# A two-block transformer forward pass on one core, with and without the products of zeros at its stage boundaries

## What is computed

```python
for layer in range(2):                               # first block
    h = rmsnorm(x, norm_mix)
    qkv, gates = split(h @ w_in)
    o = [window_attention(qkv), stick_breaking(qkv), moba(qkv)]
    x = x + sum(sigmoid(g + b) * (o_i @ w_branch_i)) @ w_out
    h = rmsnorm(x, norm_ffn)
    u_a, u_v = split(causal_conv(h @ w_up))
    x = x + (silu(u_a) * u_v) @ w_down
x = rmsnorm(x, norm_final)
for l in range(2):                                   # second block
    mix = concat(retention(x), mla_attention(x), mlstm(x)) @ w_out_2
    x = layer_norm(alpha * x + mix)
    f = swiglu(x) if l == 0 else moe_swiglu(x)       # 8 experts, top 2
    x = layer_norm(alpha * x + f)
```

## Time and profile before

| | us |
|---|---|
| median of 3 runs | 2707.37 |
| the runs | 2696.85, 2707.37, 2708.14 |
| the profiled execution, from first to last instruction | 2697.0 |

### The profile page before, as it was taken

One profiled execution on the slowest core, in us unless ns is written; L12 is line 12 of the kernel. 1 busy time (PEld: TensorE's weight loads), 2 busy tenths in 40 slices (PEclk: granted clock), 3 DMA queues, 4 the chain that ended last, 5 costly groups with the idle time before them and its releaser, 6 DMA issues.

```text
span 2697.0 us, 38879 instructions
## 1 busy us (share of the span) xinstructions
PE 2569.2 (95%) x13770; PEld 2161.1 (80%) x13770; DVE 1873.7 (69%) x2141; ACT 1443.7 (54%) x1434; POOL 36.6 (1%) x46
## 2 busy tenths in 40 slices
PE   8979999998899999999999988999999999999997
PEld 7758799896688998868998767878787878788785
DVE  4536688745466876745445647888888888888888
ACT  4454444444544443533433434767677777776764
POOL 0010000000000000000000000000000000000000
PEclk9989999998899999979999788999999999999999
DMA  6305545441254554423553225989898989898986
GB/s 255 141 20 199 187 174 186 155 168 67 100 197 157 188 186 162 153 78 135 184 184 137 94 78 202 369 313 375 316 368 323 348 324 356 328 345 335 341 336 261
DMA packets 81898, 595.27 MB, mean 221 GB/s; under 512 B 9088, under 2 KB 9232, under 8 KB 10256
## 3 DMA queue, kind: packets, MB, share of 16 engines
q1 hardware_dynamic: 80624, 583.64, 58.3%
q0 software_dynamic: 1184, 10.45, 1.0%
HBM read 593.01 MB, written 1.05 MB: 220 GB/s over the span
## 4 chain that ended last, share of the span: by engine, by line
issue 69%; PE 24%; DVE 3%; DVEq 1%; ACT 1%; POOL 1%; DMA 0%; ACTq 0%; POOLq 0%
PE bank L291 6%; PE bank L292 6%; PE bank L293 6%; PE bank L377 2%; DVEq L571 1%; DVE w_lo L579 1%; PE bank L402 1%; PE bank L387 1%; DVE probs L642 0%; ACT w_hi L459 0%; DVE x_tok L1741 0%; POOL probs L738 0%; PE bank L403 0%; PE bank L337 0%; POOL small L730 0%
## 5 line engine op out<-in xcount | busy, mean ns | idle before, releaser
L579 DVE TENSOR_TENSOR w_lo<-raw,w_hi 128x2048 fp32r<-128x2048 f32 x550 | 1249.4, 2290 | 431.6 <-ACT w_hi L459 391.9
L459 ACT CAST w_hi<-raw 128x2048 fp32r<-128x2048 f32 x550 | 1050.4, 1913 | 506.9 <-PE bank L293 494.3
L291 PE MATMUL bank<-w_hi,hT_hi 128*128 128x512 f32 (+3 forms) x1360 | 538.1, 396 | 19.1 <-DVE w_lo L579 12.5
L293 PE MATMUL bank<-w_hi,hT_lo 128*128 128x512 f32 (+3 forms) x1360 | 526.1, 387 | 0.0
L292 PE MATMUL bank<-w_lo,hT_hi 128*128 128x512 f32 (+3 forms) x1360 | 525.6, 386 | 0.0
L291 PE MATMUL bank<-hT_hi,w_hi 128*128 128x256 f32 (+1 forms) x1568 | 451.1, 288 | 5.1 <-DVEq L597 4.5
L293 PE MATMUL bank<-hT_hi,w_lo 128*128 128x256 f32 (+1 forms) x1568 | 445.1, 284 | 0.0
L292 PE MATMUL bank<-hT_lo,w_hi 128*128 128x256 f32 (+1 forms) x1568 | 445.1, 284 | 0.0
L291 PE MATMUL bank<-w_hi,oT_hi 128*128 128x512 f32 x876 | 343.2, 392 | 6.7 <-DVE oT_lo L1077 3.6
L292 PE MATMUL bank<-w_lo,oT_hi 128*128 128x512 f32 x876 | 342.2, 391 | 0.0
L293 PE MATMUL bank<-w_hi,oT_lo 128*128 128x512 f32 x876 | 341.7, 390 | 0.0
(11 more groups left out here) (263 smaller groups left out, 1931.5 us busy)
## 6 DMA issues: line engine op xcount, KB each, us to landing
raw<-in_weights_dram SPq DMA_DIRECT2D x554, 1024.0 KB, 5.5
arena<-in_norms_dram POOLq DMA_DIRECT2D x2, 2048.0 KB, 8.1
arena<-in_b_gate_dram POOLq DMA_DIRECT2D x2, 1536.0 KB, 7.0
tables<-in_tables_b_dram POOLq DMA_DIRECT2D x1, 1216.0 KB, 6.2
x_tok<-in_x_dram SPq DMA_DIRECT2D x1, 1024.0 KB, 5.1
arena<-in_norm_final_dram POOLq DMA_DIRECT2D x2, 512.0 KB, 7.7
out_dram<-x_tok SPq DMA_DIRECT2D x2, 512.0 KB, 2.6
tables<-in_tables_a_dram POOLq DMA_DIRECT2D x1, 768.0 KB, 9.8
```

The source lines that it names most:

```text
L291: mm(out, st[0], mv[0], start=start, stop=False, skip_group_check=True)
L293: return mm(out, st[1], mv[0], start=False, stop=stop, skip_group_check=True)
L459: self.isa.copy(m.w_hi[:, slot, :], m.raw[:, raw, :]).then_inc(m.hi_ready, 1)
L579: self.isa.tensor_tensor(m.w_lo[:, slot, :], m.raw[:, raw, :], m.w_hi[:, slot, :].bitcast(F32), ALU.subtract).then_inc(m.lo_ready, 1)
```

## The change

`stay_warm` and its four calls are left out, with the constant that sets its length. Over an execution that is 260 products of zeros fewer on TensorE (8 times 30, 2 times 10). TensorE goes straight on to the wait for `nat_ready`. The wait for bank 0, which `stay_warm` made, is made by the transposes. Nothing else moves, on TensorE or on another engine.

```diff
-WARM = 30
 COUNT = 12
 HALF = 56
...
-    def stay_warm(self, n=WARM):
-
-        bank, zeros = self.bank(0), self.m.zeros[:]
-        for _ in range(n):
-            self.isa.matmul(bank, zeros, zeros.unsqueeze(1).to_broadcast([P, 4, P]), start=True, stop=True)
-        self.known.add(0)
-
     def turn_x(self, ident):
 
         m = self.m
-        self.stay_warm()
         banks = [self.bank(b) for b in range(4)]
         for t in range(TT):
...
         oT = (m.oT_hi, m.oT_lo)
 
-        self.stay_warm()
         self.eng.wait_ge(m.nat_ready, w.next(m.nat_ready, 2))
         self.turn_rows(m.nat, (0, 1, 2, 3), ident)
         self.coming = {0, 2, 4, 6}
...
             self.used(self.rows(outs, self.chunk(), 512, branch, 4, 0, 4))
-        self.stay_warm(WARM // 3)
         self.eng.wait_ge(m.nat_ready, w.next(m.nat_ready))
         self.turn_rows(m.nat, (0, 1, 2, 3), ident)
         self.coming = {0, 2, 4, 6}
         self.project((2, 2, 1, 1, 1, 1))
 
-        self.stay_warm()
         self.eng.wait_ge(m.nat_ready, w.next(m.nat_ready, 2))
         self.turn_rows(m.nat, (0, 1, 2, 3), ident)
         self.coming = {0, 2, 4, 6}
```

## The result

| | before | changed |
|---|---|---|
| median of 17 runs, us | 2698.43 | 2712.91 |
| lowest and highest | 2693.61 to 2708.26 | 2709.74 to 2715.04 |
| profiled execution, us | 2697.0 | 2709.6 |
| ratio | | 1.0044 (95%: 1.0034 to 1.0054) |

The changed kernel is slower, by 9 to 15 us. That is between two fifths and two thirds of the 23.1 us that I forecast. The rest of the gap between 2730.5 and 2712.9 is the base: the median of three runs that I added my sum to, 2707.37, lay 9 us above the median of seventeen. By the measure that the prediction set itself (0.5%, 13.5 us) a ratio of 1.0044 is still no change, to which it gave 0.19; but the interval leaves out 1.

The account below looks back on a forecast made before the run. TensorE was taken to set the pace behind a restart; slow-clock costs of 10.8 + 2.2 + 6.0 + 2.5 + 0 + 1.6 = 23.1 us on a 2707.37 us median gave 2730.5 us (forecast 2725 to 2736, overall range 2712 to 2741).

Parts of the forecast that it names:

- restarts 1 and 4: Starts of first-block layers: first product no earlier, since it waits for copied columns; slow first chunk costs 1.1 us each.
- 2 and 5: Before the output projection: slower transposes 1.1 us, then half-clock products 2.3 us; taken as 3.0 us each.
- 3 and 6: Before the first block's feed-forwards: first product 3.2 us later, then 2.2 us in slow products; 5.4 us each.
- 5.0 us of dense products at half clock per restart: Time the clock stays low in real products once work returns, between 3.4 and 6.8 us.
- The sign that I named: In the profile after, a granted clock of 0.50 over each of restarts 2 to 7 for 7 to 10 us.
- 7: First second-block restart: second transpose group late by 1.0 us, slow chunk 1.6; 2.6 us, less 0.1 direct gain.
- 9: Second block: clock had fallen anyway before the second group of transposes, so removing the zeros costs 0.
- Restart 8: Second block: clock had fallen anyway despite the zeros, so cost 0; its 4.7 us of slow products served as evidence.
- restart 10: Router: some 13 small products take 1.3 us more and the transposes 0.3; 1.6 us.
- the program's start: Evidence for slow clock recovery: 15 products of 512 columns took 6.30 us, read as 6.2 us of half clock.
- rival (C): Clock returns before the first real product, as transposes and accumulators count as work; 7.9 us, 2715 in all; chance 0.10.

Follow-up runs that it names:

- refitted: Kernel before; no zeros at 1 and 4, 16 at 2 and 5, 28 then early accumulators at 3, 6, 8, 36 at 9 and 10, 12 between token tiles: 2702.5 us.
- before_b: The kernel before, unchanged, profiled a second time: 2706.62 us.
- before_c: The kernel before, unchanged, profiled a third time: 2703.43 us.
- only_ff: Changed kernel with the zeros put back only at restarts 3 and 6, before the first block's two feed-forwards: 2708.97 us (1.0027).
- mixer_zeros: Kernel before plus 16 products of zeros in each second-block mixer, right ahead of the latent attention's scores: 2702.94 us (1.0014).
- after_mixer: Changed kernel plus 16 products of zeros in each second-block mixer, right ahead of the latent attention's scores: 2713.3 us (1.0050).

## Why the prediction was right or wrong

**Direction and mechanism: right.** The zeros were no wait for anybody; restarts 1 and 4 start their products no later than before; the clock falls in the bare waits of 5 us and more at restarts 3, 4 and 6 to 10, and, but for one fall inside the wait, within 1.2 us of the end of the 3.8 us at 2 and 5; TensorE is the bound behind 2, 3, 5 and 6 (in the kernel before only from the fourth pair of hT_lo on, as refitted shows), so the loss stays, and zeros put back at 3 and 6 alone took back the 2.4 us at each. The transposes are slow at half clock, 3.32 us for 16 where the earlier trace rows had 1.62 for 8, against 1.72 at full clock. The Trainium skill states that the full clock does not engage for transposes ("TensorE: Matmul & The Clock Gate", "Part 4: PE-mode transpose"); the 1.72 and the 3.32 us speak against it.

**The size: wrong.** 23.1 us were forecast, and the places come to half of it. The failing step is the term "5.0 us of dense products at half clock per restart". It stood for 2.2 us at 3 and 6 each, and none was paid there. In its place the half clock ended while the accumulators ran, so that these cost 0.8 us more than at full clock instead of 1.6; the transposes cost their 1.6 as forecast. At 2 and 5 the term stood for 2.3, of which 1.0 was paid (2.1 us of half clock), and the transposes' 1.1 shrank to 0.1, because the clock fell only while they ran. The sign that I named, half clock for 7 to 10 us over each of restarts 2 to 7, held at 3 and 6 (10.2) and nearly at 7 (6.8); at 2 and 5 it was 3.4 us (once 6.8), at 4 twice 3.4 with full clock between.

| restart | forecast | measured | half clock in real products |
|---|---|---|---|
| 3 and 6 | 5.4 each | 2.4 each | 5.0 forecast, 0 measured |
| 2 and 5 | 3.0 each | 1.1 each (once 2.2) | 5.0 forecast, 2.1 measured |
| 1 and 4 | 1.1 each | 0.4 and 0.5 in the mean | 3.4 and 3.4 measured, mostly while TensorE waits for hT anyway |
| 7 | 2.5 | 0.9 up to the first product and none behind it; the stage lies within before's scatter | 0.9 measured |
| 8 | 0 | 0 or 4.1, by whether the zeros held | |
| 9 | 0 | 0 | |
| 10 | 1.6 | 1.4 against the first profile, 0 against before_b and before_c | |

Without 8 and 10 the lines add up to about 9 us. Restart 8 adds 2, as of the six profiles of kernels with the plain zeros three held the clock and three did not, and restart 10 up to 1.4: 11 to 12, against 9 to 15 measured.

I took the 5.0 from restart 8 (4.7 us) and from the program's start (6.2). Neither was like 3 and 6. At 3 and 6 one group of 16 transposes comes without a pause, and the clock is back 5.1 us behind the first of them, with 10.24 us of half clock in all of which half is the wait. At restart 8 the rows come in two groups with idle between, and the half clock lasted 3.8 to 4.7 us into the products in the profiles of before and of the changed kernel that lost the clock. That the two groups make the difference isn't shown: in only_ff the clock was back 1.8 us ahead of the first product behind the same two groups. There it had fallen 2.6 us behind the stage's start, in the changed kernel 3.0 us; so a shift of 0.4 us of the work against the clock's changes may be what decides, but no run sets it. My rival (C), "the clock comes back before the first real product", is what happens at 3 and 6; I gave it 0.10 and spoke against it with restart 8, the wrong witness. Its 7.9 us are close to the sum of the table partly by luck: it had 1.5 each at 3 and 6, where 2.4 was paid. And its 2715 comes near 2712.9 only on a base that was 9 us too high.

**Restart 8 and the base.** I took one execution for the rule twice: that "the clock had fallen anyway" at 8 (it hadn't in two of three profiles of before), and that the median of three runs, 10 us above the profile, was the level to add to. The three runs already spread over 11 us, which was reason enough to put the base lower.

**Restart 10.** Here the sum was right for the one profile that it was read from. In the changed kernel the small products run 0.21 us apart from the first on, and the 13th stands 1.4 us later in its stage than in that profile, against 1.6 forecast. But in before_b and before_c the clock fell 1.6 us behind the first transpose, in spite of the zeros, and the products came as late and as slowly as in the changed kernel. Before_b:

```profile
1624.47 0.34 PE L291 MATMUL bank<-w_hi,hT_hi 128*128 128x8 f32 x1 [1.20 <-DVEq L597]
1624.67 0.35 PE L292 MATMUL bank<-w_lo,hT_hi 128*128 128x8 f32 x1
```

## What to carry to other kernels

Filling a wait with useless products pays where TensorE is the bound behind the wait, and only what it saves there: here 0.9 to 2.4 us at the five places where it pays every time, 0.4% in all. To price a fall of the clock, look for a place in the trace with the same pattern of waits and work, not only the same length of idle, and ask whether what comes first behind it (transposes, openings of accumulators) takes the slow time before the long products start. And where one kernel's profiles differ from each other by stage, one of them says little about what an edit costs in those stages: take three, and compare stages rather than totals.

## What the runs showed of the hardware

Products with 64 or 32 of 128 rows kept TensorE busy for 30 us at half clock without the clock coming back (the first profile of before); when it had come up in a burst of zeros, it fell 4.9 us into them (mixer_zeros, 1152.32 to 1157.19) and 5.7 us into them (after_mixer). In the four bursts of 16 full products issued at half clock, the clock was up 3.5 and 2.2 us behind the start of the burst in mixer_zeros, and 5.0 and 1.9 us behind it in after_mixer. Of the seven waits of 1.8 us between dense products in the experts, three were followed by a fall of the clock in the first profile of before, two in before_b and five in mixer_zeros, each time for 3.4 us.
